# Turning MLP activations and residual blocks by VectorE squares and on-chip transfers in place of TensorE transposes

## The reference

```python
def sq_relu_mlp(h, w_up, w_down):
    return jnp.square(jax.nn.relu(h @ w_up)) @ w_down        # 2048 -> 8192 -> 2048

def reference(x, ...):
    h = x                                                    # (1, 256, 2048)
    for l in range(2):
        if l < 1:
            h = h + mamba2_mixer(rms_norm(h, ssm_norm_w[l]), ...)      # w_in 2048x10304, w_out 4096x2048
        else:
            k, v = shared_kv(h, kv_norm_w, w_kv, k_norm_w)             # w_kv 2048x4096
            h = h + diff_attention(rms_norm(h, attn_norm_w[0]), k, v, w_q[0], ..., w_o[0], ...)
        h = h + sq_relu_mlp(rms_norm(h, mlp_norm_w[l]), w_up[l], w_down[l])
    return h
```

## Time and profile before

| | |
|---|---|
| time, median of 3 runs | 2549.83 us |
| profiled execution: its time | 2549.55 us |
| profiled execution: span from first to last instruction | 2547.9 us |
| TensorE matmuls busy | 2524.6 us, 12081 instructions |
| VectorE busy | 1477.1 us, 1508 instructions |
| ScalarE busy | 1194.0 us, 1460 instructions |
| DMA | 468.14 MB, mean 184 GB/s |
| mean granted TensorE clock | 0.999 |

### The profile page before, as it was taken

One profiled execution on the slowest core, in us unless ns is written; L12 is line 12 of the kernel. 1 busy time (PEld: TensorE's weight loads), 2 busy tenths in 40 slices (PEclk: granted clock), 3 DMA queues, 4 the chain that ended last, 5 costly groups with the idle time before them and its releaser, 6 DMA issues.

```text
span 2547.9 us, 33913 instructions
## 1 busy us (share of the span) xinstructions
PE 2524.6 (99%) x12081; PEld 2117.9 (83%) x12081; DVE 1477.1 (58%) x1508; ACT 1194.0 (47%) x1460; POOL 210.2 (8%) x115
## 2 busy tenths in 40 slices
PE   8999999999999999999999999999999999999999
PEld 7888888888888888888888888888888888888887
DVE  5777777775555555555555655666555555555554
ACT  5455555554444344344344545555544444443443
POOL 2433233330000000000000000000000000000000
PEclk9999999999999999999999999999999999999999
DMA  7555555554566565666665565554565666666664
GB/s 220 171 181 181 176 178 171 175 180 167 182 198 182 193 191 184 193 187 190 191 187 182 178 203 167 164 176 162 174 194 188 189 189 190 190 184 195 190 187 167
DMA packets 266592, 468.14 MB, mean 184 GB/s; under 512 B 17198, under 2 KB 50320, under 8 KB 265472
## 3 DMA queue, kind: packets, MB, share of 16 engines
q1 hardware_dynamic: 264736, 457.87, 58.6%
q0 software_dynamic: 1472, 8.79, 1.0%
q10 hardware_dynamic: 288, 0.11, 0.0%
HBM read 464.54 MB, written 2.16 MB: 183 GB/s over the span
## 4 chain that ended last, share of the span: by engine, by line
PE 88%; DVE 4%; issue 2%; POOL 2%; DMA 2%; ACT 2%; DVEq 0%; SPq 0%; ACTq 0%; POOLq 0%
PE acc L366 25%; PE acc L368 25%; PE acc L367 25%; PE aux L366 2%; PE aux L374 2%; PE aux L367 2%; PE aux L368 2%; DVE w_lo L1093 2%; DMA work<-decay_rows 1%; POOL work L1543 1%; POOL work L1541 1%; DVE work L1180 1%; ACT w_hi L739 1%; PE aux L435 1%; PE aux L434 1%
## 5 line engine op out<-in xcount | busy, mean ns | idle before, releaser
L1093 DVE TENSOR_TENSOR w_lo<-w_raw,w_hi 128x1024 fp32r<-128x1024 f32 x865 | 1121.4, 1301 | 821.4 <-ACT w_hi L739 819.9
L739 ACT ACTIVATE w_hi<-w_raw 128x1024 fp32r<-128x1024 f32 x865 | 913.3, 1060 | 1007.5 <-PE acc L368 904.6
L366 PE MATMUL acc<-w_hi,stationary 128*128 128x512 f32 x3200 | 1256.5, 393 | 1.9 <-DVE w_lo L1093 0.7
L368 PE MATMUL acc<-w_hi,stationary 128*128 128x512 f32 x3200 | 1246.4, 389 | 0.0
L367 PE MATMUL acc<-w_lo,stationary 128*128 128x512 f32 x3200 | 1245.7, 389 | 0.0
L368 PEld LDWEIGHTS acc<-w_hi,stationary 128*128 128x128 f32 x3200 | 600.6, 188 | 125.8
L366 PEld LDWEIGHTS acc<-w_hi,stationary 128*128 128x128 f32 x3200 | 601.0, 188 | 124.5 <-issue 1.1
L367 PEld LDWEIGHTS acc<-w_lo,stationary 128*128 128x128 f32 x3200 | 601.2, 188 | 121.2
L1487 POOL TENSOR_TENSOR small<-small 128x2 f32<-128x2 f32 (+2 forms) x22 | 38.3, 1744 | 1207.2 <-DVE small L1103 1207.2
L366 PE MATMUL aux<-w_hi,stationary 128*128 128x256 f32 (+1 forms) x384 | 123.8, 322 | 3.4 <-DVE w_lo L1093 3.4
L368 PE MATMUL aux<-w_hi,stationary 128*128 128x256 f32 (+1 forms) x384 | 122.2, 318 | 0.0
(11 more groups left out here) (173 smaller groups left out, 929.4 us busy)
## 6 DMA issues: line engine op xcount, KB each, us to landing
w_raw<-in_w_up SPq DMA_DIRECT2D x256, 512.0 KB
w_raw<-in_w_down SPq DMA_DIRECT2D x256, 512.0 KB
w_raw<-in_ssm_w_in SPq DMA_DIRECT2D x129, 512.0 KB
w_raw<-in_ssm_w_out SPq DMA_DIRECT2D x64, 512.0 KB
w_raw<-in_w_kv SPq DMA_DIRECT2D x64, 512.0 KB
w_raw<-in_ssm_w_in SPq DMA_DIRECT2D x64, 256.0 KB
w_raw<-in_w_q SPq DMA_DIRECT2D x32, 512.0 KB
w_raw<-in_w_o SPq DMA_DIRECT2D x32, 512.0 KB
```

Source lines behind the costliest of these rows:

```text
L366: pe.matmul(o, xh, hi[:, k], start=start, stop=False)
L368: mm = pe.matmul(o, xl, hi[:, k], start=False, stop=stop)
L739: a.activation(whi[:, s, :], raw[:, s, :], ACT.Copy).then_inc(sem("hi_made"), 1)
L1093: v.tensor_tensor(wlo[:, s, :], raw[:, s, :], whi[:, s, :].bitcast(F32), ALU.subtract).then_inc(sem("lo_made"), 1)
```

## The change

TensorE's 44 turns (352 transposes) go. In their place VectorE transposes the block within 32x32 squares, in one instruction (`turn`), from `act` or from the residual `h` into `blocks_t`. This leaves each square turned, but in the wrong group of 32 partitions. SP then issues 16 transfers from SBUF to SBUF (`spread`), one for each pair of a source and a destination group of 32 partitions: 32 partitions x 2 x 128 numbers (32 KB), in runs of 512 bytes. The result stands in `channels`, with the four channel tiles interleaved, so `up_hi` and `up_lo` become four instructions of 128x256 each, as `resid_hi` and `resid_lo` were, and read SBUF in place of PSUM. Both buffers use space that belongs to the attention's `kT` and `qT`; there is one of each, so the next `turn` waits for the last `spread`, and the next `spread` for the last low part.

SP's `spread` stands ahead of the load of piece 7 of a block. ACT's and DVE's steps on the turned block move from behind piece 5 to behind piece 6 (7 in the mixer's output product, 30 in place of 29 for one in the product with `w_o`). SP's loops of the MLPs are written out.

```diff
+            def spread(n):
+
+                sp.wait_ge(sem("turned"), n)
+                wait(sp, sem("turned_lo"), n - 1)
+                for b in range(4):
+                    for q in range(4):
+                        src = blocks_t[32 * b:32 * b + 32, q * 2 * P:(q + 1) * 2 * P].rearrange("c (t f) -> c t f", t=TT)
+                        dst = channels[32 * q:32 * q + 32, :].rearrange("c (t b f) -> c t b f", t=TT, b=4)[:, :, b]
+                        sp.dma_start(dst, src).then_inc(sem("spread"), 16)
...
+                def chunk(c, first, last):
+                    pos = Pos(base, c, PER_CHUNK)
+                    n = c * 4 + T
+                    for u in range(4):
+                        blocks(pos, 8 * u, up, c * D + u * NB, 8, steps=turn_at_7(n + u if u or first else None))
+                    for d in range(4):
+                        carried = T_carry + d if last and T_carry is not None else None
+                        blocks(pos, 32 + 8 * d, down, d * NB, 8, c * KT, turn_at_7(carried if d else n + 4))
...
-                        if j == 2 and u > 0:
-                            turn_up(c, u - 1)
-
-                def turn_up(c, u):
-                    pe.wait_ge(sem("up_read"), c * 4 + (U + u + 1))
-                    pe.wait_ge(sem("turned_lo"), c * 4 + (T + u - 1))
-                    transposes(to_channels(aux[u % 2]), lambda i, t: act[:, t, i * P:(i + 1) * P]).then_inc(sem("turned"), 1)
...
                 def up_hi(c, u):
-                    a.wait_ge(sem("turned"), c * 4 + (T + u + 1))
-                    a.activation(st[:, RB + 4 * u:RB + 4 * u + 4, 0, :], whole(aux[u % 2]), ACT.Copy).then_inc(sem("turned_hi"), 1)
+                    a.wait_ge(sem("spread"), c * 1024 + (T + u + 1) * 256)
+                    for i in range(4):
+                        ins = a.activation(tokens(st[:, RB + 4 * u + i, 0, :]), channel_tile(i), ACT.Copy)
+                    ins.then_inc(sem("turned_hi"), 1)
...
-                        if j == 5:
+                        if j == 6:
                             up_hi(c, u)
...
+            def turn(src, n):
+
+                wait(v, sem("spread"), (n - 1) * 256)
+                v.transpose(blocks_t.rearrange("p (q t k i) -> p t k q i", q=4, k=4, t=TT),
+                            src.rearrange("p t (k q i) -> p t k q i", k=4, q=4)).then_inc(sem("turned"), 1)
...
                     v.scalar_tensor_tensor(act, acc[u % 2][:, :, :], 0.0, act, ALU.max, ALU.mult).then_inc(sem("up_read"), 1)
+                    v.wait_ge(sem("up_read"), c * 4 + (U + u + 1))
+                    turn(act, c * 4 + (T + u + 1))
...
-                        if j == 5:
+                        if j == 6:
                             up_lo(c, u)
```

More of the change, by code:

```diff
@@ L273, in load, with blocks @@
                     sp.dma_start(dst[:, c], src).then_inc(sem(f"raw_in{pos.slot(off)}"), 32 // len(parts))
-            def blocks(pos, off, w, n0, pieces, k0=0):
+            def blocks(pos, off, w, n0, pieces, k0=0, steps=None):
                 if not isinstance(n0, int):
@@ L316, in mlp, with resid_turn, steps @@
+            out_w = ssm_w_out[0].rearrange("(k p) n -> p k n", p=P)
+            def resid_turn(n):
+                def steps(j):
+                    if j == 7:
+                        spread(n)
+                return steps
+            blocks(Pos(OUT0), 0, out_w, 0, 16)
+            for n in range(1, 4):
+                blocks(Pos(OUT0), n * 16, out_w, n * NB, 16, steps=resid_turn(T_OUT + n))
+            def mlp(layer, base, T, T_carry):
                 up = w_up[layer].rearrange("(k p) n -> p k n", p=P)
@@ L317, in mlp, with turn_at_7, steps @@
                 down = w_down[layer].rearrange("(k p) n -> p k n", p=P)
[L318 to L324, removed]
+                def turn_at_7(n):
+                    def steps(j):
+                        if j == 7:
+                            spread(n)
+                    return steps if n is not None else None
@@ L325, in _, with pair, steps @@
+                for c in range(4):
+                    chunk(c, c == 0, c == 3)
+            mlp(0, UP0, T_MLP0, T_MLP0_END)
             kv = w_kv.rearrange("(k p) n -> p k n", p=P)
             wq = w_q[0].rearrange("(k p) n -> p k n", p=P)
-            with sp.Fori(0, 4) as j:
+            def pair(j, first):
                 pos = Pos(ATT0, j, PER_PAIR)
-                blocks(pos, 0, kv, j * NB + D, 8)
+                def steps(i):
+                    if i == 7:
+                        spread(T_MLP0_END + 4)
+                blocks(pos, 0, kv, j * NB + D, 8, steps=steps if first else None)
@@ L594, in mlp @@
                     for d in range(4):
-                        down(c, d, c == 3 and T_carry is not None)
-            mlp(UP0, R_MLP0, T_MLP0, 0, T_MLP0_END)
+                        down(c, d)
+            mlp(UP0, R_MLP0, T_MLP0, 0)
             def turn_q(r):
@@ L662, in pair @@
                     piece(pos, i, ps, NB, region + 2 * (i % 8), i % 8 == 0, i % 8 == 7)
-                    if i == 2 and first:
-                        turn_resid(3, R_WO, None)
                     if i == 22:
@@ L1020, in pair @@
                         resid_squares(3, R_WO)
-                    if first and i == 5:
+                    if first and i == 6:
                         resid_hi(3, T_MLP0_END + 4, to_att)
@@ L1409, in pair @@
                         add_resid(3, Pos(UP0, 3, PER_CHUNK), PER_CHUNK - 1, True)
-                    if first and i == 5:
+                        turn_resid(3, R_WO, T_MLP0_END + 4)
+                    if first and i == 6:
                         resid_lo(3, T_MLP0_END + 4, to_att)
```

87 lines of the change are left out of this document (43 added, 44 removed).

## The result

The changed kernel takes **2664.03 us** (median of 4 runs, 2658.45 to 2667.2); the kernel before, beside it, 2549.86. The ratio is 1.0444, 95% interval 1.0431 to 1.0456: 4.4% slower, where 2517 us was forecast, 1.3% faster. The profiled execution took 2665.54 us, its span 2663.9. The time lies far outside the range. The cause is the one that rival B names, issues on SP that take longer than reckoned, at a price within the bounds given for it; most of the loss came in another place than rival B gives.

A forecast was written before the change was run, and what follows sets the result against it. TensorE, busy 99% of the span, was taken to bound the kernel. From 2549.55 us, 39.1 saved, 2.4 charged for fourth blocks and 4.5 for the residual blocks and `w_o` gave 2517 us; range 2510 to 2542.

The forecast's parts named there:

- rival B: SP issues in order, so sixteen slow issues delay the weight load behind them: 2569 us at 0.60 each; chance 0.10.
- What goes: 44 turns of eight transposes leave TensorE's stream, at 0.89 us a turn: 39.1 us saved.
- The transpose: VectorE's new transpose of 128x1024, assumed to take 1.22 us like its other passes over as many elements.
- Rival A: VectorE's transpose is slow, 2.42 us at GpSimd's pace: 2524 to 2542 us; chance 0.25.
- SP's issue: Sixteen transfers issued by SP at 0.46 us each, 7.4 us a turn; upper bound 0.74 each.
- the prediction's own loop: Start of SP's transfers, sixteen issues, load burst and rounding: 21.4 us against a block of 21.76, called the tightest place.
- B+20.0: The prediction's clock: microseconds after a block ends on TensorE; piece 7's low part was forecast at 17.2, needed at 19.0.
- M: Theory of the follow-up experiments: the turned block lands late, delaying piece 7's rounding and low part queued behind its copies.
- Fourth blocks: A chunk's fourth turned block, needed ahead of piece 6 of the first down block: 0.3 us charged, 8 times, 2.4 us.
- Residual blocks and `w_o`: Late turned blocks at the attention's residual blocks and in the product with `w_o`: 4.5 us charged together.
- Bytes at nothing: The DMA's extra 23 MB ride beside the weight loads and were costed at nothing.
- C: Rival: the burst of loads refills slower than profiled, 2549 to 2561 us; chance 0.05 near no change.

The follow-up runs named there:

- run 1: The changed kernel with four transfers of 128 partitions per turn in place of sixteen of 32, same bytes, turned data left out: 2510.29 us.
- run 11: The changed kernel with its sixteen transfers reading HBM in place of SBUF, same count, shapes and bytes, turned data left out: 2531.93 us.
- run 3: The changed kernel with 12 of the 16 transfers per turn, a quarter of each block left out: 2532.65 us.
- run 9: The kernel of run 8 with turns 21 to 27 (attention's start, product with `w_o`) back on TensorE, nothing left out: 2516.42 us.
- run 2: The changed kernel with all sixteen transfers per turn, each moving half its bytes, half the turned data left out: 2654.07 us.
- run 8: The changed kernel regrouping through HBM by SP: four writes ahead of the load of piece 7, two reads behind it, nothing left out: 2529.43 us.

## Why the prediction was wrong, and where it was right

- **What goes: right.** 39.1 us of transposes; run 1 comes out at 2510.29, 39.7 below its kernel before.
- **The transpose: right.** 1.25 us against 1.22. Rival A is out. The Trainium skill, "VectorE: DVE Perf Modes", section "The three transpose paths", has 311 ns for 128x128 bf16, from which the prediction had estimated 2.5 us for eight; this instruction takes half of that, and the measurement decides.
- **SP's issue: the step that failed.** The prediction said "I take 0.46, the spacing of small ones in a row". Those read HBM. Run 11 shows 0.46 for just that, and the change shows 0.64 for SBUF to SBUF: 10.2 to 10.5 us in place of 7.4. Run 3, with twelve issues, wins back 131 of the 147 us by which the forecast missed, and run 11, with all sixteen at 0.46, 132. The text had placed the turning point, where the gain is used up, at 0.57 us and the upper bound at 0.74; between them lay the truth, and rival B got 0.10. The range even stopped at 2542, though its bounds reached to 2667. And by the prediction's own loop the loss begins much nearer to the 0.46: its 0.36 us of room over sixteen issues are used up at 0.48 us each.
- **Rival B: right in the cause, not in the place, and too small.** By its working 0.64 gives a loop of 3.7 + 10.2 + 9.3 + 1.0 = 24.2, 2.4 over a block, 24 x 2.44 = 59, and piece 7 at B+20.0, 1 us late 20 times: 2517 + 79 = 2596. It put three quarters of this on the late load of piece 10, to be seen as a late ReLU. In the trace that is rare: only in two of the 32 blocks does ReLU start about 1 us late, as here, where the last matmul of the block starts at 1018.40 (in the kernel before ReLU starts 0.4 us behind it):

```profile
1018.91 1.06 ACT L757 ACTIVATE w_hi<-w_raw 128x1024 fp32r<-128x1024 f32 x1 [0.17 <-DMA w_raw<-in_w_down]
1019.88 1.00 ACT L938 ACTIVATE work<-acc 128x1024 f32<-128x1024 f32 x1
```

  The stall came earlier, ahead of piece 7, 2.4 us long; it makes the block 21.8 + 2.4 = 24.2 us, as long as the loop, so that piece 10 is then in time (an estimate from these terms). Missing in B are the half clock (31 us by the tally), a load of piece 7 that takes 1.0 us longer from issue to rounding, and M: ScalarE stands at the turned block (204.5 us), which the working of B left out. In the change's own trace the shares can be told apart for the MLPs: of the 58 us ahead of piece 7 the wait for the load holds 43, and the other 15 would be left by M with the load in time (an estimate from the same rows); the 17 ahead of piece 6 are the turned block alone. For the other 38 us, most of them at the residual blocks and in the product with `w_o`, the shares are not told apart.
- **Fourth blocks: too small.** 0.3 us each were charged; 16.2 us in 8 waits came, from the issues. With the issues as reckoned, 1.0 us in two waits is left (run 3), less than was charged.
- **Residual blocks and `w_o`: too small, by 9 us.** 2.5 + 2 were charged; run 3 has 6.6 + 6.9. Two turns two pieces apart make one gap of 6.5 rather than 2. The working had the second transpose wait for the first spread (5.0 us of wait in run 3), but not that the second spread then waits for the first turn's low parts: in run 3 that transpose starts at 1781.55, its first transfer only at 1786.70, and its copies at 1795.65, 14 us behind the transpose in place of 9. (The 1.9 us charged at the attention's start are 2.1 by the printed terms, 18.4 - 16.3; it changes nothing.) Run 9 takes these turns back to TensorE and gets all of it.
- **Bytes at nothing: right** with four transfers (run 1); with sixteen, half of them gave 10 us back (run 2).
- **C**, the slow refill: not what happened. The loads behind the transfers are late mainly because they are issued late: of the 4.2 us by which the rounding of piece 7 comes later than reckoned, 3.2 are the issue and 1.0 the load.

## What to carry to other kernels

Count the DMA issues on a queue as work of that engine, priced by a row of their own form (ends, shape, partitions): here the forms lay between 0.43 and 0.60 us on SP. A wide transfer cost about as much to issue as a narrow one, so on SP fewer, wider ones won even by way of HBM and with more bytes. Where a plan has a turning point a quarter above an assumed price (0.57 against 0.46) and no row shows that very form, the range must reach to the other side. A stall on TensorE can bring half clock behind it (here 0.27 us for each us of gap, on average), and a wait in an in-order queue is charged with all that stands behind it.

## What the runs showed of the hardware that was not expected

- Issue by SP, per transfer of 32 partitions: 0.60 us SBUF to SBUF, 0.43 from HBM, 0.43 to HBM (run 8, of 128 KB); ScalarE 0.62; GpSimd 0.53, steady (533 to 634 ns), but 4.1 us to landing against 1.9.
- 128 partitions in one transfer: 0.62 us to issue and 2.2 to land SBUF to SBUF (run 1), 0.59 and 3.8 from HBM (run 8, 256 KB).
- STREAM_TRANSPOSE of 128x1024 fp32, in 32x32 squares: 1.25 us, like any pass over 1,024 elements here.
- The granted clock fell to half behind 20 of 46 gaps of TensorE in the change, and the length of the wait does not sort them: one of 1.77 us had it, one of 3.23 us had not. Over the run, 113 us of gaps brought 31 us of steps at half clock.
